# Weights of each dense phase of a hybrid decoder trunk land in up to 16 places, and PE waits for them piece by piece in a first tile written apart

## The chip, the cores and the metric

The kernel runs on one core of one Trainium2 chip. The metric is the device time of one execution in microseconds; before the change the median of three runs is 3684.71 us (3683.56 to 3687.84).

## What is computed

One inference step of a two-layer decoder trunk, for a prompt of 2048 rows and a sample group of 8x8 rows with the same weights, all in float32. With D = 1024, cut to what matters:

```python
for i in range(2):
    u = rms_norm(h, norm_w[i])
    if i == 0:
        z = u @ w_in_even            # 1024 x 4616: q, k, v, forget, rq, rk, rv, gate
        m = even_out(fox_attention(z), retention(z), gate) @ w_out_even
    else:
        xb, g = split(u @ w_in_odd)  # 1024 x 2048
        m = (rg_lru(conv(xb)) * silu(g)) @ w_out_odd
    h = h + m
    e = rms_norm(p[i] @ ple_proj[i], ple_norm_w[i])
    h = h + sigmoid(h @ ple_gate_w[i]) * e
y = rms_norm(h, final_norm_w)
```

The outputs are y, the new keys, values and forget values, and the new retention, recurrent and convolution states.

## The kernel before, in words

The trunk runs phase after phase, with a barrier of all engines between two: the input projection in two halves (`in_proj`, tiles named `in`), sample retention, attention, retention, the tail of layer 0 (`tail`), the recurrent layer (`lru`), and the tail of layer 1. The order within a phase is the order in which each engine's code is written; there is no scheduler. SP issues nearly all transfers, from one queue.

Rows are worked through in T = 17 tiles of 128 (16 of the prompt, one of the sample). `each_tile` (L101) runs a step for each: a hardware loop over pairs of tiles, then the last three (in the second half seven) written out. `lru` is written out whole, in groups of 512 rows, the sample's 64 rows first.

Every float32 product is made of three: the operands are cut into a high and a low part, and `split3` (L125 to L127) adds high by high, high by low and low by high. The weights are cut on the chip by `SplitWeights` (L130). A piece is 128 rows by 512 columns, 256 KB. SP loads piece n into place n modulo the number of places, and first waits until the piece that was there has been cut (L149); ACT writes the high part (`make_high`, L154), DVE the low part (`make_low`, L159) and counts `low`, on which PE waits. In `in_proj` there are four column groups of eight pieces, so 32, and eight places; in the tail of layer 0 the projection and output weights are held from earlier and the 16 gate pieces use four places lent by `u_hi` and `u_lo`; in the tail of layer 1 there are 4 + 16 + 16 pieces and six places; in `lru` 16 pieces and eight places at the start (later ones come during the run).

In tile 0 of `in_proj` PE takes the groups in turn and for each waits for all eight of its pieces. In the first half, x must first be normalised (`norm`, by ACT and DVE), turned (`turn`, L692, by PE through `ps_t`) and cut; tile t+1 is normalised by ACT and DVE at the head of step t, and turned by PE between groups 1 and 2. Group 2 there also holds the eight forget columns, which ACT and DVE cut last of all (`wf_split`). The first matmul group of a tile needs the bank that the evacuation of the tile before has emptied: in the second half DVE's rotary (L642 to L647) empties group 0's. There POOL multiplies the last gate by `gn`, and side work on forget values (`GatesAside`) has constants of its own.

In the tails DVE adds the output product to h (`add_out`, L2421) after it has cut the first eight gate pieces, and PE turns the sum (L2515). In `lru` ACT works out a softplus of lambda (L2787 to L2791), which needs the constants, before it cuts weights; then it copies the sample's rows (`keep_rows`, L2798), PE turns them, and `keep` (L2805) takes up the first channel block.

## Time and profile before

| | |
|---|---|
| median of the timed runs | 3684.71 us (3683.56 to 3687.84) |
| the profiled execution | 3673.12 us |
| its span, first to last instruction | 3671.4 us |
| PE busy | 3268.0 us (89%), 22374 matmuls |
| DVE, ACT, POOL busy | 1719.6, 1281.3, 294.9 us |
| HBM traffic | 172 GB/s over the span |
| mean granted PE clock | 0.943 |

The profile is of one execution; its span leaves out 1.7 us around the first and the last instruction. PE is the matmul engine, PEld its weight loads, DVE, ACT and POOL the elementwise engines, SPq the queue from which SP issues transfers. PEclk is the clock that was granted to PE as a share of full speed. A window's busy time is what an engine worked in that stretch; where a row ends in brackets, they hold the engine's idle time before it and what ended it.

### The profile page before, as it was taken

Reading aid. Unit: us, or ns where it says so; the run is one execution under the profiler, and the core shown is the slowest. Engines: PE = TensorE matmul, PEld = TensorE weight load, DVE = VectorE, ACT = ScalarE, POOL = GpSimd, SP = SyncE. Lnnn points to the kernel's source line nnn. Section 1 sums busy time; section 2 is a strip of 40 time slices with the busy share of each in tenths; the row PEclk is TensorE's granted clock in tenths of the full one; section 3 lists DMA queues with packets and bytes.
Section 4 is the critical chain, followed back from the end, with each engine's and each line's share of the span. In section 5 each row is a group of like instructions: output and inputs, shape, how many; then the busy total and the mean of one; then the engine's idle time right before and its main releaser. Section 6 shows DMA issues by size and latency. Waiting matters only on the chain. (4 is left out here: it accounts for less than half of the span.)

```text
span 3671.4 us, 63114 instructions
## 1 busy us (share of the span) xinstructions
PE 3268.0 (89%) x22374; PEld 2483.7 (68%) x22374; DVE 1719.6 (47%) x2974; ACT 1281.3 (35%) x2326; POOL 294.9 (8%) x306
## 2 busy tenths in 40 slices
PE   6999789996699999999996859999869999499998
PEld 5888678884465565556554747888757677378887
DVE  3222231142776677667652753333346676433333
ACT  3111121120134334334333533333356666533232
POOL 0000000011211111111100530000000000000000
PEclk9999899996699999999998979999989999699999
DMA  5444652344688898789866863333244433332221
GB/s 146 139 139 139 192 138 93 108 140 123 221 289 287 271 316 282 266 285 320 282 216 205 292 240 120 113 121 123 98 170 138 129 132 106 120 116 89 80 89 59
DMA packets 381250, 636.26 MB, mean 173 GB/s; under 512 B 138697, under 2 KB 201201, under 8 KB 364594
## 3 DMA queue, kind: packets, MB, share of 16 engines
q1 hardware_dynamic: 361730, 496.54, 41.0%
q0 software_dynamic: 19264, 136.46, 10.6%
q8 instruction: 143, 2.34, 0.3%
q14 instruction: 113, 0.93, 0.1%
HBM read 488.74 MB, written 144.13 MB: 172 GB/s over the span
## 5 line engine op out<-in xcount | busy, mean ns | idle before, releaser
L125 PE MATMUL in_ps_z<-in_w_hi,in_u_hi 128*128 128x512 f32 x952 | 374.9, 394 | 43.3 <-DVE in_w_lo L159 43.3
L126 PE MATMUL in_ps_z<-in_w_lo,in_u_hi 128*128 128x512 f32 x952 | 373.4, 392 | 0.0
L127 PE MATMUL in_ps_z<-in_w_hi,in_u_lo 128*128 128x512 f32 x952 | 373.2, 392 | 0.0
L1521 DVE STREAM_TRANSPOSE att_samp_kt<-att_samp_k_ring 128x1024 f32<-128x1024 f32 x256 | 306.9, 1225 | 24.5 <-DMA att_samp_k_ring<-cache_k,att_samp_rows_now 12.3
L1676 PE MATMUL att_fox_ps_o<-att_fox_prob,att_fox_v_one 128*65 128x512 f32 (+3 forms) x640 | 290.3, 537 | 10.1 <-ACT att_fox_prob L1377 9.8
L1377 ACT ACTIVATE att_fox_prob<-att_fox_ps_k 128x512 f32<-128x512 f32 (+1 forms) x320 | 167.4, 531 | 243.0 <-DVE att_fox_ps_k L1489 156.5
L125 PEld LDWEIGHTS in_ps_z<-in_w_hi,in_u_hi 128*128 128x128 f32 x952 | 180.6, 190 | 82.3 <-issue 28.7
L125 PE MATMUL tail_ps_g<-tail_wg_hi,tail_h_hi 128*128 128x512 f32 x544 | 216.5, 398 | 13.9 <-DVE tail_p_lo L2405 9.8
L1470 DVE TENSOR_REDUCE att_fox_part_max<-att_fox_ps_n 128x1 f32<-128x512 f32 (+2 forms) x320 | 193.4, 604 | 72.1 <-PE att_fox_ps_n L1643 63.0
L127 PE MATMUL tail_ps_g<-tail_wg_hi,tail_h_lo 128*128 128x512 f32 x544 | 212.9, 391 | 0.0
L126 PE MATMUL tail_ps_g<-tail_wg_lo,tail_h_hi 128*128 128x512 f32 x544 | 212.9, 391 | 0.0
L127 PEld LDWEIGHTS in_ps_z<-in_w_hi,in_u_lo 128*128 128x128 f32 x952 | 180.6, 190 | 38.0
L126 PEld LDWEIGHTS in_ps_z<-in_w_lo,in_u_hi 128*128 128x128 f32 x952 | 180.7, 190 | 36.9
L1302 POOL DMA_INDIRECT att_samp_k_ring<-cache_k,att_samp_rows_now x128 | 121.0, 946 | 750.6 <-DVE att_samp_kt L1521 683.7
L2433 DVE SCALAR_TENSOR_TENSOR tail_e<-tail_ps_g,tail_e 128x512 f32<-128x512 f32 x68 | 47.0, 692 | 278.7 <-ACT tail_ps_g L2366 278.7
L1660 PE MATMUL att_fox_ps_k<-att_fox_q_a,att_fox_k_a 128*128 128x512 f32 (+1 forms) x320 | 167.6, 524 | 9.4 <-issue 7.1
L1733 PEld LDWEIGHTS att_samp_ps_v<-att_samp_v_ring,att_samp_prob_t 128*16 128x16 f32 x4096 | 102.7, 98 | 74.2 <-issue 65.0
L1707 PE MATMUL att_samp_ps_s<-att_samp_kt,att_samp_q_blocks 128*32 128x128 f32 x4096 | 149.2, 290 | 0.0
L1707 PEld LDWEIGHTS att_samp_ps_s<-att_samp_kt,att_samp_q_blocks 128*32 128x32 f32 x4096 | 111.5, 115 | 50.9 <-issue 48.7
L1733 PE MATMUL att_samp_ps_v<-att_samp_v_ring,att_samp_prob_t 128*16 128x128 f32 x4096 | 140.8, 279 | 4.0 <-DMA att_samp_v_ring<-cache_v 4.0
L1642 PE MATMUL att_fox_ps_n<-att_fox_k_a,att_fox_q_a 128*128 128x512 f32 (+2 forms) x320 | 127.0, 397 | 19.3 <-DVE att_fox_part_max L1470 16.0
L125 PEld LDWEIGHTS tail_ps_g<-tail_wg_hi,tail_h_hi 128*128 128x128 f32 x544 | 102.7, 189 | 48.1 <-DVE tail_h_lo L2426 21.3
(385 smaller groups left out, 6835.9 us busy)
## 6 DMA issues: line engine op xcount, KB each, us to landing
att_samp_v_ring<-cache_v SPq DMA_DIRECT2D x512, 256.0 KB
tail_a_hi<-a_hi SPq DMA_DIRECT2D x34, 512.0 KB, 5.9
tail_a_lo<-a_lo SPq DMA_DIRECT2D x34, 512.0 KB, 6.2
in_w_stage<-w_in_even SPq DMA_DIRECT2D x64, 256.0 KB, 6.7
lru_u_hi<-u_hi SPq DMA_DIRECT2D x8, 2048.0 KB, 8.0
lru_u_lo<-u_lo SPq DMA_DIRECT2D x8, 2048.0 KB, 13.0
in_x<-x SPq DMA_DIRECT2D x17, 512.0 KB, 3.5
u_hi<-in_u_hi SPq DMA_DIRECT2D x17, 512.0 KB, 3.8
```

Of the source, the lines that this page charges most:

```text
L125: pe.matmul(out, act_hi, w_hi, start=start, stop=False)
L126: pe.matmul(out, act_hi, w_lo, start=False, stop=False)
L127: return pe.matmul(out, act_lo, w_hi, start=False, stop=stop)
L1302: pool.indirect_dma_start(k_ring[:, n % KR, :], None, io["cache_k"], bass.IndirectOffsetOnAxis(ap=rows_now[:, par, n:n + 1], axis=0)).then ...
L1377: act.activation(prob[:, s % 4, r:G], ps_k[:, s % 2, r:G], ACT.Exp).then_inc(exped.sem, 1)
L1470: dve.tensor_reduce(part_max[:, g, b % B4, c:c + 1], ps_n[:, 0:w], AX.X, ALU.max).then_inc(maxed.sem, 1)
L1521: ins = dve.transpose(kt[:, n % 2, :, :].rearrange("p c (s i) -> p s c i", s=SLOTS)[:, p * two:(p + 1) * two], k_ring[:, n % KR, p * two * ...
L1642: pe.matmul(ps_n[:, 0:w], q_a[:, par, q], k_a[:, par, k], start=True, stop=False)
L1660: pe.matmul(ps_k[:, s % 2, r:G], k_a[:, par, k], q_a[:, par, q], start=True, stop=False)
L1676: pe.matmul(ps_o[0:HD + 1, r:G], v[:, par, kt, :], prob[:, s % 4, r:G], start=kt == 0, stop=kt == B4 * (g + 1) - 1).then_inc(weighed.sem, 1)
L1707: last = pe.matmul(ps_s[h * QUAD:(h + 1) * QUAD, at:at + PAGE], q_blk[:, bpar, block, :], kt[:, y, block, :], start=False, stop=y == 1 and ...
L1733: last = pe.matmul(acc[a * QUAD:a * QUAD + 2 * NS, :], prob_t[:, c % 2, at:at + 2 * NS], v_ring[:, y, p, a * P:(a + 1) * P], start=c == 0 ...
```

## The change

It does the following, in the five dense phases:

- `in_proj`: the weights get 16 places instead of 8. In the first half 12 are their own and four are the buffer `z`, in the second eight are their own and eight are `z`, `gate_half` and `gate_tanh`. ACT and DVE wait for all pieces (`all_made`) before they write these buffers.
- SP issues tile 0's rows ahead of the constants, tile 1's rows after the first eight pieces, and gn and the side work's constants last. b_forget gets its own semaphore.
- Tile 1's norm is done by ACT and DVE after the first 16 pieces.
- PE waits for each piece by itself in tile 0, and no more in later tiles. For that, PE's tiles 0 and 1 are written apart, ahead of the loop (`apart=1`); in the first half ACT's and DVE's too.
- `tail`: identity and p first, with the identity on its own semaphore; the two norm weights after tile 0's rows; in layer 0 six places for the gate weights instead of four; PE's waits per piece, and tiles 0 and 1 apart.
- `lru`: 16 places, eight of them working buffers; rows first, then all 16 pieces, then the constants; the weights are cut ahead of the softplus; the later pieces count on semaphores of their own.

The core of the diff:

```diff
@@ each_tile
-def each_tile(eng, step, tiles=T, unroll=2, peel=3):
+def each_tile(eng, step, tiles=T, unroll=2, peel=3, apart=0):
-    with eng.Fori(0, pairs) as i:
+    for t in range(2 * apart):
+        step(t, t // 2, t % 2)
+    with eng.Fori(apart, pairs) as i:
@@ SplitWeights
+    def all_made(self, eng):
+        eng.wait_ge(self.low, len(self.pieces))
@@ in_proj
-        weights = SplitWeights(ph, pieces, 8)
+        idle = [z[:, g, :] for g in range(GN)] + ([] if first else [b[:, g, :] for b in (half_z, tanh_z) for g in range(2)])
+        weights = SplitWeights(ph, pieces, 12 if first else 8, idle)
@@ in_proj, sync
-            if first:
-                sp.dma_start(ident[:, :], io["identity"]).then_inc(consts_in, 16)
-                sp.dma_start(nw[:, :], io["norm_w"][0:1, :].broadcast_to([P, D])).then_inc(consts_in, 16)
-                sp.dma_start(bf[:, :], io["b_forget"][0:1, :].broadcast_to([P, H])).then_inc(consts_in, 16)
-            else:
-                sp.dma_start(gn[:, :], io["ret_gn_w"][0:1, :].broadcast_to([P, W])).then_inc(consts_in, 16)
...
             fetch(0, 0)
+            if first:
+                sp.dma_start(nw[:, :], io["norm_w"][0:1, :].broadcast_to([P, D])).then_inc(consts_in, 16)
+                sp.dma_start(ident[:, :], io["identity"]).then_inc(consts_in, 16)
             weights.load(sp, 0, KC)
+            fetch(1, 1)
+            weights.load(sp, KC, 2 * KC)
+            if first:
+                sp.dma_start(bf[:, :], io["b_forget"][0:1, :].broadcast_to([P, H])).then_inc(bf_in, 16)
+                sp.dma_start(wf_st[:, :, :], w_in[:, :, 3 * W:3 * W + H]).then_inc(wf_in, 16)
+            weights.load(sp, 2 * KC, GN * KC)
             if not first:
+                sp.dma_start(gn[:, :], io["ret_gn_w"][0:1, :].broadcast_to([P, W])).then_inc(consts_in, 16)
                 side.load(sp)
-            fetch(1, 1)
-            if first:
-                sp.dma_start(wf_st[:, :, :], w_in[:, :, 3 * W:3 * W + H]).then_inc(wf_in, 16)
-            weights.load(sp, KC, GN * KC)
@@ in_proj, scalar
-            weights.make_high(act, 0, GN * KC)
+            weights.make_high(act, 0, 2 * KC)
+            if first:
+                norm(1, 0, 1)
+            weights.make_high(act, 2 * KC, GN * KC)
             if first:
                 split_forget_act(act)
-            each_tile(act, step, peel=PEEL)
+            weights.all_made(act)
+            each_tile(act, step, peel=PEEL, apart=int(first))
@@ in_proj, vector
-            weights.make_low(dve, 0, GN * KC)
+            weights.make_low(dve, 0, 2 * KC)
+            if first:
+                norm(1, 0, 1)
+            weights.make_low(dve, 2 * KC, GN * KC)
             if first:
                 split_forget_dve(dve)
-            each_tile(dve, step, peel=PEEL)
+                dve.wait_ge(bf_in, 16)
+            weights.all_made(dve)
+            each_tile(dve, step, peel=PEEL, apart=int(first))
@@ in_proj, tensor
+            def piece_made(t, g, k):
+                if isinstance(t, int) and t == 0:
+                    pe.wait_ge(weights.low, g * KC + k + 1)
             def group(t, par, g):
-                pe.wait_ge(weights.low, (g + 1) * KC)
...
                     for k in range(KC):
+                        piece_made(t, g, k)
-            each_tile(pe, step, peel=PEEL)
+            each_tile(pe, step, peel=PEEL, apart=1)
@@ tail
-            gate_weights = SplitWeights(ph, more, 0, us)
+            gate_weights = SplitWeights(ph, more, 2, us)
...
-            for dst, src in [(ident[:, :], io["identity"]), (nw_e[:, :], io["ple_norm_w"][layer:layer + 1, :].broadcast_to([P, D])),
-                             (nw_u[:, :], next_w.broadcast_to([P, D]))]:
-                sp.dma_start(dst, src).then_inc(consts_in, 16)
...
             fetch_p(0, 0)
+            sp.dma_start(ident[:, :], io["identity"]).then_inc(ident_in, 16)
             fetch_p(1, 1)
             if not kept:
                 weights.load(sp, 0, PROJ)
             fetch(0, 0)
+            fetch_norms()
@@ tail, vector
-            dve.wait_ge(consts_in, 48)
...
+            dve.wait_ge(consts_in, 32)
             norm_e(0, 0, 0)
@@ tail, tensor
-            pe.wait_ge(consts_in, 48)
+            pe.wait_ge(ident_in, 16)
-                    if not kept:
-                        pe.wait_ge(weights.low, PROJ + (g + 1) * KC)
                     for k in range(KC):
+                        if not kept and isinstance(t, int) and t == 0:
+                            pe.wait_ge(weights.low, PROJ + g * KC + k + 1)
...
-            each_tile(pe, step)
+            each_tile(pe, step, apart=1)
@@ lru
-        weights = SplitWeights(ph, pieces, 8)
+        weights = SplitWeights(ph, pieces, LB, [b[:, 0:G] for b in (tr, ti, tg, th, sq, q, root, bx)])
...
-            sp.dma_start(chan[:, :, 0:8], io["channel"]).then_inc(consts_in, 16)
-            for n, name in enumerate(["gate_r_w", "gate_i_w"]):
-                sp.dma_start(gates[:, n], io[name][0:BH].rearrange("b d e -> d b e")).then_inc(consts_in, 16)
-            sp.dma_start(ident[:, :], io["identity"]).then_inc(consts_in, 16)
-            sp.dma_start(past_x[:, :, :, :], io["past_x"]).then_inc(consts_in, 16)
-            sp.dma_start(past_h[:, :, :], io["past_h"]).then_inc(consts_in, 16)
...
-            weights.load(sp, 0, 4)
             fetch(0, 0)
-            weights.load(sp, 4, 2 * KC)
+            weights.load(sp, 0, 2 * KC)
+            sp.dma_start(ident[:, :], io["identity"]).then_inc(consts_in, 16)
+            sp.dma_start(chan[:, :, 0:8], io["channel"]).then_inc(consts_in, 16)
+            sp.dma_start(past_x[:, :, :, :], io["past_x"]).then_inc(consts_in, 16)
+            sp.dma_start(past_h[:, :, :], io["past_h"]).then_inc(consts_in, 16)
+            for n, name in enumerate(["gate_r_w", "gate_i_w"]):
+                sp.dma_start(gates[:, n], io[name][0:BH].rearrange("b d e -> d b e")).then_inc(consts_in, 16)
             fetch(1, 1)
@@ lru, scalar
+            weights.make_high(act, 0, 2 * KC)
             act.wait_ge(consts_in, 96)
...
-            weights.make_high(act, 0, 2 * KC)
+            keep_rows(0)
             act.wait_ge(ready, 2)
-            keep_rows(0)
+            weights.all_made(act)
             keep(0, 0, 0, 0)
@@ lru, vector
+            weights.make_low(dve, 0, 2 * KC)
             dve.wait_ge(consts_in, 96)
...
-            weights.make_low(dve, 0, 2 * KC)
@@ lru, tensor
-                    pe.wait_ge(weights.low, (n + 1) * KC if t == 0 else 4 * KC)
+                    if t:
+                        pe.wait_ge(weights.low, 4 * KC)
                     for k in range(KC):
+                        if t == 0:
+                            pe.wait_ge(weights.low, n * KC + k + 1)
```

Three places in the order of the instructions. SP, start of the first half of the input projection, before (`in_w_stage` is the places of their own, `in_x` and `in_cos_sin` a tile's rows, `in_wf_stage` the forget columns):

```order
L494 DMA in_ident<-identity 128x128
L495 DMA in_norm_w<-norm_w 128x1024
L496 DMA in_b_forget<-b_forget 128x8
L503 DMA in_x<-x 128x1024
L507 DMA in_cos_sin<-cos_sin 128x64
L149 DMA in_w_stage<-w_in_even 128x512 x8
L503 DMA in_x<-x 128x1024
L507 DMA in_cos_sin<-cos_sin 128x64
L515 DMA in_wf_stage<-w_in_even 128x8x8
L149 DMA in_w_stage<-w_in_even 128x512 [waits in0_w_low_made] x24
```

and now:

```order
L508 DMA in_cos_sin<-cos_sin 128x64
L512 DMA in_norm_w<-norm_w 128x1024
L513 DMA in_ident<-identity 128x128
L151 DMA in_w_stage<-w_in_even 128x512 x8
L504 DMA in_x<-x 128x1024
L508 DMA in_cos_sin<-cos_sin 128x64
L151 DMA in_w_stage<-w_in_even 128x512 x4
L151 DMA in_z<-w_in_even 128x512 x4
L518 DMA in_b_forget<-b_forget 128x8
L519 DMA in_wf_stage<-w_in_even 128x8x8
L151 DMA in_w_stage<-w_in_even 128x512 [waits in0_w_low_made] x12
L151 DMA in_z<-w_in_even 128x512 [waits in0_w_low_made] x4
```

Tile 0's x (L504) stands ahead of these; sixteen pieces are issued before the first that waits, where there were eight. ACT in the same place, from the cut of tile 0's u on, before:

```order
L572 CAST in_u_hi<-in_ps_t 128x1024
L154 CAST in_w_hi<-in_w_stage 128x512 x16
L154 CAST in_wv_hi<-in_w_stage 128x512 x8
L154 CAST in_w_hi<-in_w_stage 128x512 x8
L550 CAST in_wv_hi<-in_wf_stage 128x8x8
```

and now:

```order
L579 CAST in_u_hi<-in_ps_t 128x1024
L159 CAST in_w_hi<-in_w_stage 128x512 x12
L159 CAST in_w_hi<-in_z 128x512 x4
L570 ACTIVATE in_ps_t,in_stat<-in_x 128x1024
L572 ACTIVATE in_stat<-in_stat 128x1
L159 CAST in_wv_hi<-in_w_stage 128x512 x8
L159 CAST in_w_hi<-in_w_stage 128x512 x4
L159 CAST in_w_hi<-in_z 128x512 x4
L557 CAST in_wv_hi<-in_wf_stage 128x8x8
```

The two instructions of tile 1's norm (L570, L572) now stand after the sixteenth piece; before, they came in the loop behind the forget columns. ACT at the start of the recurrent layer, before:

```order
L2787 ACTIVATE lru_soft<-lru_channel 128x8
L2789 ACT_TABLE_LOAD
L2789 ACTIVATE lru_soft<-lru_soft 128x8
L2791 ACT_TABLE_LOAD
L2791 ACTIVATE lru_soft<-lru_soft 128x8
L154 CAST lru_w_hi<-lru_w_stage 128x512 x16
L2798 COPY lru_new_rows<-lru_ps_x 64x512
L2798 COPY lru_new_rows<-lru_ps_g 64x512
L2805 COPY lru_xb<-lru_ps_x 128x8x8
```

and now, from the last three pieces on:

```order
L159 CAST lru_w_hi<-lru_minus_one_less 128x512
L159 CAST lru_w_hi<-lru_root 128x512
L159 CAST lru_w_hi<-lru_gated_x 128x512
L2817 ACTIVATE lru_soft<-lru_channel 128x8
L2819 ACT_TABLE_LOAD
L2819 ACTIVATE lru_soft<-lru_soft 128x8
L2821 ACT_TABLE_LOAD
L2821 ACTIVATE lru_soft<-lru_soft 128x8
L2828 COPY lru_new_rows<-lru_ps_x 64x512
L2828 COPY lru_new_rows<-lru_ps_g 64x512
L2835 COPY lru_xb<-lru_ps_x 128x8x8
```

The casts of the sixteen pieces now come ahead of the softplus, and the row copies behind it.

## Rows read from the trace of the kernel before

**Rows 1.** Part 1 of the page: busy us (share of the span), instructions.
```profile
PE 3268.0 (89%) x22374; PEld 2483.7 (68%) x22374; DVE 1719.6 (47%) x2974; ACT 1281.3 (35%) x2326; POOL 294.9 (8%) x306
```

**Rows 2.** Windows, first half's start: stretch, length, PE, PEld, DVE, ACT, POOL, PEclk, DMA, GB/s.
```profile
7.00:15.00 8.00, 1.94 (x8) 1.57 (x8) 1.60 (x3) 2.66 (x5) 0.00 (x0) 1.00 1.00 363
15.00:19.00 4.00, 0.00 (x0) 0.00 (x0) 2.98 (x5) 4.00 (x7) 0.00 (x0) 1.00 0.11 24
19.00:31.00 12.00, 8.54 (x24) 6.48 (x24) 7.22 (x12) 5.11 (x10) 0.00 (x0) 1.00 0.97 172
31.00:37.00 6.00, 3.75 (x16) 3.11 (x17) 5.03 (x8) 4.96 (x9) 0.00 (x0) 1.00 1.05 390
37.00:47.00 10.00, 1.98 (x9) 1.31 (x7) 5.86 (x9) 5.19 (x9) 0.00 (x0) 0.75 1.01 186
```

**Rows 3.** Timelines of DVE and PE there: start us, us, operation [idle before <-releaser].
```profile
48.27 0.69 DVE L159 TENSOR_TENSOR in_w_lo<-in_w_stage,in_w_hi 128x512 fp32r<-128x512 f32 x1 [0.44 <-ACT in_w_hi L154]
...
51.64 1.97 PE L692 MATMUL in_ps_t<-in_ident,in_xn 128*128 128x128 f32 x8 [12.65 <-DVE in_xn L624]
...
54.05 0.42 PE L125 MATMUL in_ps_z<-in_wv_hi,in_u_hi 128*128 128x260 f32 x1
54.27 0.42 PE L126 MATMUL in_ps_z<-in_wv_lo,in_u_hi 128*128 128x260 f32 x1
...
57.53 0.28 PE L127 MATMUL in_ps_f<-in_wv_hi,in_u_lo 128*128 128x260 f32 x1
57.65 0.28 PE L125 MATMUL in_ps_f<-in_wv_hi,in_u_hi 128*128 128x260 f32 x1
```

**Rows 4.** Windows, start of the projection's second half, columns as in rows 2.
```profile
439.00:442.00 3.00, 0.00 (x0) 0.00 (x0) 0.00 (x0) 0.00 (x0) 0.00 (x0) 0.50 0.93 156
442.00:447.00 5.00, 0.00 (x0) 0.00 (x0) 0.00 (x0) 0.52 (x1) 0.00 (x0) 0.50 1.04 389
...
457.00:468.00 11.00, 4.14 (x15) 3.01 (x14) 4.16 (x6) 3.71 (x6) 0.00 (x0) 0.81 1.02 163
468.00:474.00 6.00, 3.30 (x8) 2.63 (x9) 4.58 (x7) 4.79 (x8) 0.00 (x0) 0.50 1.05 381
474.00:486.00 12.00, 10.07 (x42) 7.93 (x40) 6.88 (x11) 5.75 (x10) 0.00 (x0) 0.94 0.97 171
```

**Rows 5.** Timelines of SP, PE and DVE there.
```profile
452.44 25.76 SPq L149 DMA_DIRECT2D in_w_stage<-w_in_even  x24
...
487.53 0.50 PE L125 MATMUL in_ps_z<-in_w_hi,in_u_hi 128*128 128x512 f32 x1 [3.46 <-DVE in_w_lo L159]
...
489.15 0.42 DVE L647 TENSOR_TENSOR in_z<-in_prod_cos,in_prod_sin 128x256 f32<-128x256 f32 x1
```

**Rows 6.** Timelines of PE and DVE, start of layer 0's tail; DMA issues (median to landing).
```profile
2210.22 0.49 PE L125 MATMUL tail_ps_g<-tail_wg_hi,tail_h_hi 128*128 128x512 f32 x1 [2.57 <-DVE tail_wg_lo L159]
...
2190.88 1.34 DVE L159 TENSOR_TENSOR tail_wg_lo<-tail_u_hi,tail_wg_hi 128x512 fp32r<-128x512 f32 x2 [0.58 <-ACT tail_wg_hi L154]
...
2197.26 1.33 DVE L159 TENSOR_TENSOR tail_wg_lo<-tail_u_lo,tail_wg_hi 128x512 fp32r<-128x512 f32 x2 [0.90 <-ACT tail_wg_hi L154]
...
tail_u_hi<-ple_gate_w SPq DMA_DIRECT2D x8, 256.0 KB, 3.2
```

**Rows 7.** Windows and timelines of ACT at the start of the recurrent layer.
```profile
2709.00:2722.00 13.00, 13.00 (x56) 10.74 (x56) 3.95 (x22) 5.84 (x13) 0.00 (x0) 0.92 0.94 345
...
2671.07 0.22 ACT L2787 ACTIVATE lru_soft<-lru_channel 128x8 f32<-128x8 f32 x1 [11.80 <-DMA lru_past_h<-past_h]
...
2674.24 1.64 ACT L154 CAST lru_w_hi<-lru_w_stage 128x512 fp32r<-128x512 f32 x3
...
2697.11 0.21 ACT L2805 COPY lru_xb<-lru_ps_x 128x64 f32<-128x64 f32 x1
```

**Rows 8.** Timeline of PE at the start of layer 1's tail.
```profile
3224.87 1.97 PE L2515 MATMUL tail_ps_t<-tail_ident,tail_h 128*128 128x128 f32 x8 [5.76 <-DVE tail_h L2421]
```

**Rows 9.** Part 3 of the page: DMA queue, kind: packets, MB, share of 16 engines.
```profile
q8 instruction: 143, 2.34, 0.3%
```

More of the change, by code:

```diff
@@ L575, in step @@
                 if first and not static(t + 1, LAST):
-                    norm(t + 1, i + par, 1 - par)
+                    if not (isinstance(t, int) and t == 0):
+                        norm(t + 1, i + par, 1 - par)
                     cut(t + 1, i + par, 1 - par)
@@ L650, in step @@
                 if first and not static(t + 1, LAST):
-                    norm(t + 1, i + par, 1 - par)
+                    if not (isinstance(t, int) and t == 0):
+                        norm(t + 1, i + par, 1 - par)
                     cut(t + 1, i + par, 1 - par)
@@ L2290, in _, with fetch_norms @@
             next_w = io["norm_w"][1:2, :] if first else io["final_norm_w"]
-            for dst, src in [(ident[:, :], io["identity"]), (nw_e[:, :], io["ple_norm_w"][layer:layer + 1, :].broadcast_to([P, D])),
-                             (nw_u[:, :], next_w.broadcast_to([P, D]))]:
-                sp.dma_start(dst, src).then_inc(consts_in, 16)
+            def fetch_norms():
+                for dst, src in [(nw_e[:, :], io["ple_norm_w"][layer:layer + 1, :]), (nw_u[:, :], next_w)]:
+                    sp.dma_start(dst, src.broadcast_to([P, D])).then_inc(consts_in, 16)
             def fetch_p(t, par):
@@ L2526, in gate @@
                             pe.wait_ge(*h1_low.at(t, k // 4))
+                        if isinstance(t, int) and t == 0:
+                            pe.wait_ge(gate_weights.low, OUT + g * KC + k + 1 - gate_base)
                         last = split3(pe, ps_g[:, g, :], t_hi[:, k * P:(k + 1) * P], t_lo[:, k * P:(k + 1) * P], half(wg_hi[:, k, :], g),
@@ L2614, in lru @@
         y = ph.sb("y", [P, G])
+        weights = SplitWeights(ph, pieces, LB, [b[:, 0:G] for b in (tr, ti, tg, th, sq, q, root, bx)])
+        later_in = [ph.sem(f"w_later_in{x}") for x in range(LB)]
         y_hi = ph.sb("y_hi", [P, 2, G], F32R)
```

26 lines of the change are left out of this document (15 added, 11 removed).

## The prediction

> **What bounds the kernel now.** I read the busy shares first. [rows 1] PE computes in 89% of the span, and nothing the diff touches changes how many matmuls there are or how long one takes. What can move is PE's idle time, and the edits sit at the starts of five phases, between barriers, so I went to the windows, engine timelines and waits of those starts and worked out each phase's saving by itself; a barrier keeps them apart, so they add.
>
> First half of the input projection: the DMA engines are full from 7 to 15 us, then nearly empty for 4 us (24 GB/s), because eight places hold eight pieces and SP may not issue the ninth until DVE has cut the first [rows 2]. DVE cuts the last piece at 48.27, only then come tile 1's norm and its turn (51.64), and PE starts group 2 right behind it, at 53.26, two matmuls before the 54.05 of [rows 3]. One more thing in [rows 2] shapes everything: with the engines equally full (share 0.97 to 1.05) pieces 8 to 15 and 24 to 31 arrive at 172 to 186 GB/s, pieces 16 to 23 at 390. The second half shows the same pattern: 163, 381, 171 [rows 4]. It is not the number of places: there pieces 8 to 15 could all be issued at once from 452.44 (DVE had cut the first eight by then) and still ran at 163. So a piece of an odd column group costs about 1.45 us, one of an even group 0.67, and more places do not shorten that.
>
> **The change, part by part.**
>
> *Input projection, first half.* The bytes ahead of piece 8 stay the same (x, norm weights, identity, eight pieces, second x); with 16 places piece 8 follows at once. The empty stretch goes: 19 minus 15 is 4 us, less 0.3 for the small b_forget and forget columns that now stand among the pieces, 3.7. All later pieces are paced by their transfer, so the last cut moves from 48.96 (48.27+0.69) to 45.3. Second, tile 1's norm and turn now happen after piece 15: before, PE waited for them from the cut of the forget columns, done 0.1 to 0.2 us after the last piece's, to 53.26: 4.2 us [rows 3]. Group 2 still waits for `wf_split`, which ACT and DVE reach only after all 32 pieces, so the waits per piece give nothing to groups 2 and 3, and finishing groups 0 and 1 sooner only lengthens PE's idle time before them. Its price: PE was already 1.6 us into its warm-up when group 2 began (turn from 51.64); now group 2 begins cold. A 260-column matmul follows the last after 0.22 us at the 1.2 GHz level (54.05, 54.27) and after 0.12 at 2.4 GHz (57.53, 57.65) [rows 3], so 1.6 us of it costs 0.8. Sum 3.7+4.2-0.8 = **7.1 us** (bounds 5 and 10: no warm-up help at all and a slower restart of the queue; or x, now first, bringing everything 3 us forward).
>
> *Input projection, second half.* Bytes ahead of piece 8 fall: before, gn 0.26, u 1.08, eight pieces 2.10, the side work's constants 0.85 and second u 1.08 MB, 5.4 MB, ending at 457 [rows 4]; after, 4.26 MB, at the 389 GB/s of 442 to 447 from 439.2 on, ends at 450.1. That is 6.9 us, and the rest of the stream is paced by transfer. gn and constants go behind the pieces; POOL needs gn only for the store of group 3, and fetch(2), queued behind it on SP, is wanted only by tile 2, a tile's 96 matmuls of 0.23 us or 22 us later. Then PE: group 3 now runs piece by piece. Before, it started at 487.53 and tile 1 followed 5.6 us later. After, PE is done about 1 us after the last cut, but tile 1's group 0 waits for the bank that DVE's rotary empties, 2.1 us after the last cut (to 489.57) [rows 5]. So 5.6-2.2 = 3.4 us. I take off 1.0 for a colder start of tile 1: in the first half PE worked from 51.64 on, was still at the slow pace at 54.27 and at the quick one at 57.53 [rows 3]; half of the time between is lost, 1.3 to 2.9, say 2, and I give it one chance in two. 6.9+3.4-1.0 = **9.3 us** (6 to 13).
>
> *Tail of layer 0.* Identity and p come ahead of 1 MB of norm weights, so PE starts some 4 us sooner; but that is not the limit. The turn of h1 waits for add_out on DVE, which stands behind the cut of the eighth gate piece, done at 2198.6 (2197.26+1.33), and with four places the fifth to eighth came late [rows 6]. With six, two more come without a gap, and the last two are issued at the first two cuts (2191.5 and 2192.2, from 2190.88 on) and land 3.2 us later by the median of such issues: 2195.4, cast 0.6, cut 0.7, 2196.7, so 1.9 us. The 2.57 us that PE waited for the second half of the gate weights [rows 6] goes too: six pieces lie ready behind the turn. Against it: PE, done with out_proj 4 us sooner, idles some 3.6 us before the turn. In its 12.65 us of idle time before 51.64 [rows 3] the clock fell to the 1.2 GHz level: the mean 0.75 of 37 to 47 [rows 2] puts that near 42, after 3 us. I charge 0.7. **3.8 us** (1.5 to 6).
>
> *Recurrent layer.* Before: consts, four pieces, u, then pieces at eight places, and the first keep at 2697.11, right behind the copy of g's rows [rows 7]. After: 1.05 MB of u and 4.2 MB of pieces run without a gap, at the 389 GB/s of [rows 4] from 2667.2 (1.6 us after the first issue) to 2680.7; the last is cut near 2682.3. PE follows per piece, done by 2683. Now the consts are late: 0.7 MB in short rows, landing about 2684. ACT then needs 3.2 us for the three small activations with two table loads (2671.07 to the first cast at 2674.24), and 1.1 for both row copies: first keep at 2688.6. **8.5 us** (5 to 10). What was hidden beside the loads, the softplus chain, is now in the open; without that it would be 12.
>
> *Tail of layer 1.* Places stay six and bytes ahead of w_out stay 3.8 MB. PE's early start ends in the same wait: DVE cuts the eighth gate piece, then add_out (5.76 us of waiting for PE), then the turn at 3224.87 [rows 8]. **0** (-2 to 3).
>
> Straight-line tiles 0 and 1 lengthen PE's code by a seventh (5895 rows to 6771), but add no instruction that runs. I price them at 0: all of the recurrent layer is straight-line already, and from 2709 to 2722 PE is busy in 13.00 of 13.00 us with the DMA engines at 0.94 [rows 7]. Waits of ACT and DVE on all pieces are met when they are reached; the lent buffers are first written after them.
>
> Sum: 7.1+9.3+3.8+8.5 = 28.7 us. The profiled execution took 3673.1 us and would take 3644.4; the median of the three timed runs is 3684.7, 11.6 above it, so I forecast **3656.0**.
>
> **A rule against the change.** Fed per piece, PE gets 3 matmuls (0.69 us at full pace) every 1.45 us. Before, between whole groups, it idled 12.65 us and the clock fell to half anyway [rows 2, 3]. The Trainium skill (TensorE: Matmul & The Clock Gate, HAM oscillation) describes a kernel whose every K tile started at half clock because each waited for its transfer, and advises running all K tiles before waiting again. By that rule the first tiles stay at 1.2 GHz; rival B is what it would do here, worked out from rows. No row yet shows PE fed at this pace.
>
> **Rivals.**
> A. More places raise the transfer rate, and 172 GB/s was a matter of waiting. For: the empty stretches vanish exactly there. Against: the full share, and the back-to-back issue at 452.44. Then DVE paces at 0.69 per piece. In the first half it starts near 15.5 (x, now first, brings it 1.7 us forward) and loses 3 to tile 1's norm: last cut 15.5+32x0.69+3 = 40.6. In the second the first piece lands near 444.3 (446.48, ACT's 0.52 us in the stretch to 447 [rows 4], less 2.2 for gn and the slow 439 to 442): 444.3+0.7+22 = 467. Gain (48.96-40.6)+4.2-0.8, (487.5-467)+3.4, 3.8 and 8.5, about 48: 3637. Beside it: the Trainium skill (HBM Reference, Specifications and Access) gives a core streaming alone about 425 GB/s, which the even groups approach and the odd ones do not. Chance 0.08.
> B. PE at half clock through each first tile. A matmul of 512 columns then takes 0.22x512/260 = 0.43 [rows 3], a piece 1.28: hidden at 1.45, not at 0.67. Second half: group 2 loses 3.6, tile 1 starts cold, 1 more; recurrent layer: 16x1.28 = 20.5 from the first cut near 2672, 4.5 lost; tail 0: turn and half the gate, 2.5. Gain 28.7-11.6 = 17: 3668. Chance 0.09.
> C. Slower. PE's code comes by DMA: 143 packets, 2.34 MB on queue 8 [rows 9], 16 KB each. If a block queues behind all places, it waits 16x1.45 = 23 us; once in each of three starts, 70-29 = 41 slower: 3726. It decides from a stall of 10 us per start. Against it [rows 7], as above. Chance 0.04.
> D. The gains are swallowed by a later wait, for instance the second and third tiles' inputs. Against: each such fetch hangs on tile 0's own results, so it moves with it. 3685. Chance 0.05.
>
> **How the numbers follow.** The forecast has 0.74. Its bounds taken together (the deviations are independent) give a gain of 20 to 39; B widens it to 17, part of A to 42: 3643 to 3669. About 0.2%, 7.4 us, is what a measurement of this kernel tells from nothing: faster by more 0.74+0.08+0.09 = 0.91, within 0.05, slower 0.04.
>
> **What would show it.** Right: no stretch under 100 GB/s between 7 us and the last piece; group 2 of the first half starting near 45.5; tile 1 of the second half about 9 us sooner; the stall before the second gate half in tail 0 gone; the first keep of the recurrent layer waiting on the consts and not on PE; tail 1 unchanged at its turn. Wrong: rates of the odd groups near 390 (A); the granted clock 0.5 through tile 0 and 1 (B); idle time of PE in tile 1 put down to issue (C).

## The result, and the profile after

The changed kernel takes 3655.9 us, the median of six runs (3652.7 to 3669.8), against 3684.5 before (3680.4 to 3687.8): a ratio of 0.9927, 95% interval 0.9912 to 0.9943, or 21 to 32 us. The forecast was 3656.0. The busy shares of the page, to be held against [rows 1] and [rows 9]:

```profile
PE 3279.9 (90%) x22374; PEld 2490.2 (68%) x22374; DVE 1719.5 (47%) x2974; ACT 1281.2 (35%) x2326; POOL 295.4 (8%) x306
...
q8 instruction: 153, 2.51, 0.3%
```

PE's count is the same. It is busy 12 us longer, which tells nothing yet: a second profile of the kernel before had 3285.4 us, 17 more than the first.

The total is the weakest evidence here. The profiled execution of the changed kernel spans 3654.6 us, 16.8 less than that of before, where the medians differ by 28.7. So I read each phase by itself, from SP's first issue in it to the first issue of the next. In the changed kernel these are:

```profile
429.84 0.34 SPq L506 DMA_DIRECT2D in_u_hi<-u_hi  x1
...
831.87 0.56 SPq L808 DMA_DIRECT2D prep_natural<-rq  x1
...
2161.74 0.35 SPq L2321 DMA_DIRECT2D tail_p<-p  x1
...
2652.71 0.34 SPq L2748 DMA_DIRECT2D lru_u_hi<-u_hi  x1
...
3166.63 0.34 SPq L2321 DMA_DIRECT2D tail_p<-p  x1
```

The table has the lengths in us. "Mean" is over all profiles whose code was the same in that phase: two of before, four to six with the changed kernel's code. The column of gains is the difference of the two means.

| phase | before, first profile | after, first profile | mean before | mean after | gain | forecast |
|---|---|---|---|---|---|---|
| input projection, first half | 438.1 | 429.8 | 438.1 | 430.0 | 8.1 | 7.1 |
| second half | 411.9 | 402.0 | 413.1 | 402.6 | 10.5 | 9.3 |
| sample retention to retention | 1324.3 | 1329.9 | | | | |
| tail of layer 0 | 491.2 | 491.0 | 491.7 | 489.5 | 2.1 | 3.8 |
| recurrent layer | 518.5 | 513.9 | 520.5 | 514.9 | 5.6 | 8.5 |
| tail of layer 1 | 487.3 | 488.0 | 488.3 | 488.9 | -0.6 | 0 |

The five gains add to 25.7, inside the interval of the timed runs. The stretch in the middle has the same instructions in all kernels and took between 1322 and 1340 us in the thirteen profiles. That is the noise of this kernel. It is 5.6 us of the 11.9 by which the two single profiles (16.8) fall short of the medians (28.7); most of the rest is that the first profile of before was also quick in its dense phases.

**First half.** Windows of the changed kernel, for [rows 2], columns as there:

```profile
11.00:15.00 4.00, 0.95 (x6) 0.58 (x4) 2.06 (x3) 3.10 (x6) 0.00 (x0) 1.00 1.01 330
15.00:19.00 4.00, 4.00 (x10) 3.13 (x11) 4.00 (x8) 2.69 (x5) 0.00 (x0) 1.00 1.04 182
19.00:23.00 4.00, 4.00 (x16) 3.17 (x15) 1.97 (x3) 1.38 (x3) 0.00 (x0) 1.00 1.04 151
...
27.00:31.00 4.00, 2.69 (x9) 1.45 (x9) 2.98 (x6) 3.34 (x7) 0.00 (x0) 1.00 1.06 364
...
35.00:39.00 4.00, 0.00 (x0) 0.00 (x0) 3.39 (x6) 2.07 (x4) 0.00 (x0) 0.50 0.99 175
```

The empty stretch is gone, and the pattern of slow (151 to 182 GB/s) and quick (364) column groups is as it was. Timelines of DVE and PE there, for [rows 3]:

```profile
42.78 1.36 DVE L164 TENSOR_TENSOR in_w_lo<-in_z,in_w_hi 128x512 fp32r<-128x512 f32 x2
44.06 0.22 DVE L561 TENSOR_TENSOR in_wv_lo<-in_wf_stage,in_wv_hi 128x64 fp32r<-128x64 f32 x1
...
31.73 1.10 PE L710 MATMUL in_ps_t<-in_ident,in_xn 128*128 128x128 f32 x8 [1.31 <-DVE in_xn L636]
44.38 0.56 PE L127 MATMUL in_ps_z<-in_wv_hi,in_u_hi 128*128 128x260 f32 x1 [11.55 <-issue]
```

The last piece is cut at 44.14 (42.78+1.36), 4.8 us sooner than before; group 2 follows the cut of the forget columns at once. PE idled 11.55 us ahead of it; the trace puts that down to "issue", but the cut that ends just before shows the wait.

**Second half.** Windows and PE's timeline, for [rows 4, 5]:

```profile
445.00:450.00 5.00, 2.56 (x11) 1.52 (x10) 1.90 (x3) 1.24 (x2) 0.00 (x0) 1.00 1.02 185
450.00:455.00 5.00, 3.87 (x9) 2.24 (x9) 2.08 (x3) 2.19 (x4) 0.00 (x0) 0.58 1.01 238
455.00:461.00 6.00, 5.97 (x21) 4.85 (x22) 5.67 (x9) 5.51 (x10) 0.00 (x0) 0.78 1.05 391
461.00:466.00 5.00, 4.89 (x22) 3.70 (x21) 3.15 (x5) 2.23 (x4) 0.00 (x0) 1.00 0.98 190
...
470.18 0.50 PE L127 MATMUL in_ps_z<-in_w_hi,in_u_hi 128*128 128x512 f32 x1 [0.37 <-DVE in_w_lo L164]
474.79 0.47 PE L127 MATMUL in_ps_z<-in_w_hi,in_u_hi 128*128 128x512 f32 x1 [1.55 <-DVE in_z L659]
```

Group 3 follows its pieces, and tile 1 begins when the rotary has emptied its bank (L659), as forecast: 44.95 us after the phase's start, where it was 55.

**Tail of layer 0.** PE's timeline and the windows around it, for [rows 6]; ahead of them the turn in the kernel before:

```profile
2199.84 1.10 PE L2515 MATMUL tail_ps_t<-tail_ident,tail_h 128*128 128x128 f32 x8 [1.75 <-DVE tail_h L2421]
```

```profile
2187.01 1.97 PE L2542 MATMUL tail_ps_t<-tail_ident,tail_h 128*128 128x128 f32 x8 [4.67 <-DVE tail_h L2447]
2189.72 0.77 PE L127 MATMUL tail_ps_g<-tail_wg_hi,tail_h_hi 128*128 128x512 f32 x1 [0.75 <-DVE tail_h_lo L2452]
...
2185.74:2189.74 4.00, 1.98 (x9) 1.61 (x9) 2.02 (x5) 1.31 (x3) 0.00 (x0) 0.50 0.61 210
2189.74:2193.74 4.00, 4.00 (x10) 3.17 (x11) 4.00 (x7) 2.97 (x6) 0.00 (x0) 0.50 0.37 127
2193.74:2197.74 4.00, 4.00 (x16) 3.25 (x15) 1.53 (x3) 2.52 (x3) 0.00 (x0) 0.84 0.12 37
```

The stall of 2.57 us between the gate's halves is gone, and yet the phase gained 0.2 in this profile. PE idled 4.67 us ahead of the turn, where it was 1.75; the clock stands at 0.50 through the turn, which took 1.97 us (1.10 before), and through most of the gate's first half.

**Recurrent layer.** ACT's timeline, for [rows 7]:

```profile
2660.85 5.37 ACT L159 CAST lru_w_hi<-lru_w_stage 128x512 fp32r<-128x512 f32 x8 [14.43 <-DMA lru_w_stage<-w_in_odd]
...
2673.73 0.22 ACT L2817 ACTIVATE lru_soft<-lru_channel 128x8 f32<-128x8 f32 x1 [2.02 <-DMA lru_gate_w<-gate_i_w]
...
2677.97 0.21 ACT L2835 COPY lru_xb<-lru_ps_x 128x64 f32<-128x64 f32 x1
```

The first keep hangs on the constants and the chain behind them, as forecast. It comes 25.3 us after the phase's start; before it was 31.5.

**Tail of layer 1**, PE's timeline, for [rows 8]: still the wait for `add_out`, now with 10.31 us of idle time ahead of it.

```profile
3209.13 1.97 PE L2542 MATMUL tail_ps_t<-tail_ident,tail_h 128*128 128x128 f32 x8 [10.31 <-DVE tail_h L2447]
```

### The profile page after: what moved, and what is told of

Same layout as the page of the kernel before. It is cut to its first block and busy times, and to the rows that moved or that the text cites. A ratio compares the mean times of both kernels' runs of the same rounds, so it can differ in the third digit from the quotient of the medians.

```text
span 3654.6 us, 62896 instructions
## 1 busy us (share of the span) xinstructions
PE 3279.9 (90%) x22374; PEld 2490.2 (68%) x22374; DVE 1719.5 (47%) x2974; ACT 1281.2 (35%) x2326; POOL 295.4 (8%) x306
## 5 line engine op out<-in xcount | busy, mean ns | idle before, releaser
L127 PE MATMUL in_ps_z<-in_w_hi,in_u_hi 128*128 128x512 f32 x952 | 376.3, 395 | 25.7 <-DVE in_w_lo L164 24.0
L1665 PE MATMUL att_fox_ps_n<-att_fox_k_a,att_fox_q_a 128*128 128x512 f32 (+2 forms) x320 | 127.8, 399 | 18.6 <-DVE att_fox_part_max L1493 15.1
```

Source lines behind the costliest of these rows:

```text
L127: pe.matmul(out, act_hi, w_hi, start=start, stop=False)
L1665: pe.matmul(ps_n[:, 0:w], q_a[:, par, q], k_a[:, par, k], start=True, stop=False)
```

## The experiments

All but two start from the changed kernel. Since barriers part the phases, one kernel can hold edits in several. "First output" of a tail is SP's first issue of a result of tile 0, counted from the phase's start: 44.4 and 45.3 in the two profiles of before for layer 0, 44.4 and 42.9 in the two of the changed kernel.

### The kernel before, once more

> The kernel before once more, for a second profile. The profiled execution of before was 11 us under its median. If that was a quick passage of the attention phase (in the trace of before the stretch from the start of sample retention to the start of layer 0's tail took 1324.3 us, in the changed kernel 1329.9 with the same instructions), this profile shows the five dense phases within 1 us each of the first (438.1 for the first half of the projection, 411.9 for the second, 491.2 for layer 0's tail, 518.5 for the recurrent layer, 487.3 for layer 1's tail) and the stretch between anywhere from 1320 to 1340. If instead the dense phases themselves vary by several us, the savings read phase by phase are not to be trusted.

Measured: 3687.4 us, in one run. Phases 438.1, 414.2, 492.1, 522.5, 489.4, the middle 1329.4. The first half is the same to 0.1, but the other dense phases are 0.9 to 3.9 us longer, so the 1 us that I expected was too narrow: of the 14.3 us between the two profiles 9.2 lie in the dense phases and 5.1 in the middle. A single profile shows a gain of 5 us in a phase, not one of 2; for smaller ones I use marks close to the edit, and means.

### Places as before

```diff
-        weights = SplitWeights(ph, pieces, 12 if first else 8, idle)
+        weights = SplitWeights(ph, pieces, 8)
...
-            gate_weights = SplitWeights(ph, more, 2, us)
+            gate_weights = SplitWeights(ph, more, 0, us)
...
-        weights = SplitWeights(ph, pieces, LB, [b[:, 0:G] for b in (tr, ti, tg, th, sq, q, root, bx)])
+        weights = SplitWeights(ph, pieces, LB)
```

> The changed kernel with the numbers of places of before (8, 8, 4, 8). Theory: places matter only where they close an empty stretch. First half of the projection: the ninth piece waits for the first cut, the stretch comes back, +3.7 to 4.8. Second half: the second tile's rows cover the wait, 0 to +1. Layer 0's tail: the gate pieces come in at the rate of the transfer, with six places as with four, 0. Recurrent layer: the constants now queue on SP behind pieces that wait for cuts, so the first keep comes 2 to 4 later. Sum +6 to +10, about 3664. Rival: places raise the rate at which pieces arrive; then the second half loses 5 or more as well and the sum is over 14.

Measured: 3662.1 us (ratio to the kernel before 0.9929, 0.9907 to 0.9952). First half 435.4, so +5.4 to the mean; second half 404.1, +1.5; layer 0's tail 490.2, +0.7; recurrent layer 515.6, its first keep at 26.2, which is the mean of six profiles with sixteen places (26.1). Windows and PE of the first half:

```profile
11.00:15.00 4.00, 0.95 (x4) 0.58 (x4) 2.29 (x3) 3.33 (x6) 0.00 (x0) 1.00 0.70 243
15.00:19.00 4.00, 4.00 (x10) 3.12 (x10) 3.75 (x7) 1.84 (x4) 0.00 (x0) 1.00 0.76 132
...
49.51 0.56 PE L127 MATMUL in_ps_z<-in_wv_hi,in_u_hi 128*128 128x260 f32 x1 [14.28 <-issue]
```

The DMA share falls to 0.70 and group 2 starts 5.1 us later. So the places are worth 5 us in the first half and little elsewhere. In the recurrent layer I had the mechanism wrong: SP did issue the constants 4 us later, but they landed at 22.0 us, where sixteen places gave 20.8 to 22.5, since the bytes ahead of them are the same and the stream had no gap to close.

### Whole groups

```diff
-                    pe.wait_ge(weights.low, g * KC + k + 1)
+                    pe.wait_ge(weights.low, (g + 1) * KC)
```

and likewise in both tails and the recurrent layer.

> The changed kernel with PE waiting for all eight pieces of a group, as before, all else kept. Theory: nothing in the first half (group 2 waits for the forget columns anyway), +3 in the second half (group 3 starts at the last cut, 5.2 of matmuls, of which the rotary's 2.2 were waited for anyway), 0 in layer 0's tail, +0.5 to 1 in the recurrent layer, 0 to +1 in layer 1's tail. Sum +4 (3 to 5). Rival: the waits per piece are what saves in every phase; then the first half loses 3 or more too and the sum is over 8. A second rival: PE fed per piece stays cool and whole groups are quicker; then the second half gains.

Measured: 3659.7 us (0.9923, 0.9906 to 0.9941). First half 429.5, no change; second half 404.2, +1.6; layer 0's tail 489.7, no change; recurrent layer's first keep at 28.3, +2.2; layer 1's tail 488.2. The first rival falls with the first half. The waits per piece are worth some 4 us, in these two phases alone. Both sizes were missed: +3 was expected in the second half, where tile 1 began 47.24 us after the phase's start instead of 44.9 to 46.5, and 0.5 to 1 in the recurrent layer. In the recurrent layer PE now began only with the eighth piece, after 20.76 us of idle time, at half clock, and ACT waited for it:

```profile
2677.57 0.58 ACT L2828 COPY lru_new_rows<-lru_ps_g 64x512 f32<-64x512 f32 x1 [3.28 <-PE lru_ps_g L129]
```

### Norms back

```diff
             weights.make_high(act, 0, 2 * KC)
-            if first:
-                norm(1, 0, 1)
             weights.make_high(act, 2 * KC, GN * KC)
...
+            fetch_norms()
             fetch_p(0, 0)
             sp.dma_start(ident[:, :], io["identity"]).then_inc(ident_in, 16)
...
             fetch(0, 0)
-            fetch_norms()
```

The first edit also in DVE, with the norm again in the loop's first step; the second in both tails.

> The changed kernel with tile 1's norm back in the loop (first half of the projection) and the two norm weights again ahead of identity and p (both tails). Theory for the first: group 2 starts 4.1 later (the 4.2 of the prediction), phase +4. Theory for layer 0's tail, where the change gained 0.3 instead of 3.8: PE's work on the output projection was moved early by 4 us while the turn of h1 stayed where it was, so PE idled 4.67 us ahead of it instead of 1.75, its clock fell, and the turn took 1.97 instead of 1.10 us and the gate's first half 8 instead of 6. With the norm weights ahead again PE stays at full clock: phase 2 to 3.5 us shorter. Rival: the missing 3.5 us lie in the gate pieces' arrival, and the order of the norm weights does nothing (within 0.7). Layer 1's tail: within 1.

Measured: 3657.0 us (0.9916, 0.9898 to 0.9935). The first half takes 434.0, +4.0: the norm's term of the sum, 4.2, is confirmed. Layer 0's tail takes 487.4, 2.1 less than the mean, and its first output comes at 40.8. PE and its windows there (the phase begins at 2160.62):

```profile
2185.20 1.09 PE L2534 MATMUL tail_ps_t<-tail_ident,tail_h 128*128 128x128 f32 x8 [0.78 <-DVE tail_h L2439]
2187.46 0.47 PE L127 MATMUL tail_ps_g<-tail_wg_hi,tail_h_hi 128*128 128x512 f32 x1 [1.17 <-DVE tail_h_lo L2444]
...
2180.62:2184.62 4.00, 3.79 (x17) 2.81 (x15) 2.15 (x4) 1.13 (x2) 0.00 (x0) 1.00 0.94 309
2184.62:2188.62 4.00, 2.26 (x13) 1.87 (x14) 2.63 (x5) 2.73 (x6) 0.00 (x0) 1.00 0.24 81
2188.62:2192.62 4.00, 4.00 (x20) 3.29 (x19) 3.48 (x6) 2.48 (x5) 0.00 (x0) 1.00 0.53 164
```

PE starts 4 us later, and the phase is shorter. The idle time ahead of the turn is 0.78 us, the clock stays at 1.00, the turn takes 1.09, and the gate's matmuls run at full pace. A phase that is 2 us shorter in one profile would not be enough, but the mark is: from the turn to the first output it took 16.2 us here, and 18.1 to 19.1 in the seven profiles with identity and p first and tile 1's rows in their old place. In all seven the clock fell to 0.50, for some 7 us in six and 10 in the first, behind waits of 3.1 to 5.9 us ahead of the turn. In one of them the turn itself was still quick, and the gate's matmuls were not (0.63 us each):

```profile
2183.34 1.09 PE L2542 MATMUL tail_ps_t<-tail_ident,tail_h 128*128 128x128 f32 x8 [4.16 <-DVE tail_h L2447]
```

So in layer 0's tail bringing identity and p forward moved PE's work away from the wait that it could not pass, and cooled it.

### Forget columns early

```diff
             if first:
                 norm(1, 0, 1)
+                split_forget_act(act)
             weights.make_high(act, 2 * KC, GN * KC)
-            if first:
-                split_forget_act(act)
```

and the same in DVE.

> The changed kernel with the forget columns cut right after tile 1's norm, behind sixteen pieces instead of behind all 32, in the first half of the projection. In the changed kernel PE stood idle 11.55 us ahead of group 2, waiting for them, with the last piece cut at 44.13. Theory: group 2 now runs beside the cutting and group 3 piece by piece, done 1 us behind the last cut; tile 1 starts when its rows are cut, near 46.6 instead of 57.2: phase 10 us shorter (8.5 to 11). Rival: PE, fed a piece every 1.45 us, is at half clock when tile 1 begins and the gain is 1.5 to 3 less. A second rival: the forget columns themselves land late, group 2 still waits, gain under 3.

Measured: 3647.3 us (0.9897, 0.9878 to 0.9917). The first half takes 419.1 us, 10.9 less. PE's timeline:

```profile
31.43 1.10 PE L709 MATMUL in_ps_t<-in_ident,in_xn 128*128 128x128 f32 x8 [1.29 <-DVE in_xn L635]
...
46.40 0.50 PE L127 MATMUL in_ps_z<-in_w_hi,in_u_hi 128*128 128x512 f32 x1 [1.07 <-DVE in_u_lo L641]
```

Groups 2 and 3 run beside the cutting and tile 1 begins at 46.40, at full clock. The rivals fall.

### Channel table first

```diff
+            sp.dma_start(chan[:, :, 0:8], io["channel"]).then_inc(chan_in, 16)
             fetch(0, 0)
             weights.load(sp, 0, 2 * KC)
             sp.dma_start(ident[:, :], io["identity"]).then_inc(consts_in, 16)
-            sp.dma_start(chan[:, :, 0:8], io["channel"]).then_inc(consts_in, 16)
```

ACT and DVE wait for `chan_in` alone and work out the softplus ahead of their cuts.

> The changed kernel with the recurrent layer's channel table issued first, on a semaphore of its own, and the softplus worked out ahead of the cuts, while the weights are on their way. In the changed kernel the constants landed 21.0 us after the phase's start and the chain of three activations and two table loads stood in the open behind them; PE was done with both groups of rows at 22.6. Theory: the first keep (25.3 us after the phase's start in the profile of the change, 26.8 in a later profile of the same code) comes 2 us sooner. Rival: the other constants or PE's own work are the limit and it moves by less than 0.7.

Measured: 3650.7 us (0.9922, 0.9905 to 0.9938). The phase begins at 2645.27, so the first keep is at 23.1, 3.0 sooner than the mean of 26.1. ACT and PE:

```profile
2648.24 0.21 ACT L2817 ACTIVATE lru_soft<-lru_channel 128x8 f32<-128x8 f32 x1 [9.26 <-DMA lru_channel<-channel]
...
2668.32 0.22 ACT L2836 COPY lru_xb<-lru_ps_x 128x64 f32<-128x64 f32 x1 [0.47 <-PE lru_ps_x L3020]
...
2667.88 0.27 PE L3020 MATMUL lru_ps_x<-lru_ident,lru_new_rows 64*128 64x64 f32 x1 [0.64 <-DMA lru_gate_w<-gate_i_w]
```

The softplus is hidden again. What is late next shows too: the last of the constants, the gate weights, landed 22.6 us after the phase's start, and PE waited 0.64 us for them.

### Tile 1's rows later

```diff
-            fetch(1, 1)
-            gate_weights.load(sp, OUT - gate_base, GATE - gate_base)
+            gate_weights.load(sp, OUT - gate_base, OUT + KC - gate_base)
+            fetch(1, 1)
+            gate_weights.load(sp, OUT + KC - gate_base, GATE - gate_base)
```

> The changed kernel with the rows of tile 1 (1.5 MB) issued behind the first eight gate pieces instead of ahead of them, in both tails. Theory: the turn of h1 hangs on the cut of the eighth gate piece, so 1.5 MB less ahead of it, near 390 GB/s, brings it some 3.5 to 4 us forward; in layer 0's tail PE then idles 1 us instead of 4.7 ahead of the turn and keeps its clock. First tile's output asked for 4 to 6 us sooner in layer 0's tail (44.4 in the profile of the change), 3 to 5 sooner in layer 1's (65.1). Rival: tile 1's rows are then late for the output product behind the first gate, and it all comes back there, within 1.

Measured: 3649.8 us (0.9906, 0.9889 to 0.9924). Layer 0's tail takes 484.9, 4.7 less, its first output at 38.3; layer 1's 485.1, 3.8 less, first output at 62.3 instead of 65 to 67. PE in layer 0's tail, which begins at 2164.21:

```profile
2186.35 1.10 PE L2543 MATMUL tail_ps_t<-tail_ident,tail_h 128*128 128x128 f32 x8 [1.57 <-DVE tail_h L2448]
```

The turn comes 22.1 us after the start instead of 24 to 25 and at full clock. The rows of tile 1 were not late.

### Columns exchanged

```diff
-        pieces = [(io["w_in_even"][0, k * P:(k + 1) * P, starts[g]:starts[g] + G], *weight(g, k)) ...]
+        pieces = [(io["w_in_even"][0, k * P:(k + 1) * P, starts[g ^ 1]:starts[g ^ 1] + G], *weight(g, k)) ...]
```

> The changed kernel with the weights of groups 0 and 1, and of 2 and 3, exchanged in both halves of the projection: each group reads the columns of its neighbour, so q, k, v and so on come out in each other's place. It asks what makes every second group arrive at 163 to 186 GB/s. If it is the columns (where a row's 2 KB lie in memory), the first and the third group are now the slow ones, and the first and third stretches of the windows show it. If it is the place in the stream (how much is in flight, the slots used), the second and fourth are slow as before. The times of the phases hardly move in either case, save that a slow first group delays PE's first tile.

Measured: 3654.6 us, in one run, every phase within its spread; its outputs stand in each other's place, as intended. Windows of the first half:

```profile
11.00:15.00 4.00, 1.16 (x6) 0.75 (x4) 1.76 (x3) 2.81 (x5) 0.00 (x0) 1.00 1.04 165
...
19.00:23.00 4.00, 4.00 (x16) 3.22 (x16) 2.05 (x4) 2.47 (x4) 0.00 (x0) 1.00 1.06 400
...
27.00:31.00 4.00, 2.86 (x16) 1.99 (x14) 3.34 (x7) 2.33 (x6) 0.00 (x0) 1.00 1.03 159
...
35.00:39.00 4.00, 0.00 (x0) 0.00 (x0) 2.79 (x5) 2.81 (x6) 0.00 (x0) 0.50 1.02 376
```

The slow stretches are now the first and the third, the quick ones the second and the fourth, and in the second half of the projection it is the same. So it is the columns, and not the place in the stream.

### The loop's first tiles apart, alone

```diff
-    with eng.Fori(0, pairs) as i:
+    for t in range(2 * apart):
+        step(t, t // 2, t % 2)
+    with eng.Fori(apart, pairs) as i:
```

on the kernel before, with `apart` as in the change.

> The kernel before with nothing changed but that PE's first two tiles (in the first half of the projection ACT's and DVE's too) are written out ahead of the loop. The prediction prices the longer code at nothing: every phase within 1 us of the two profiles of the kernel before, the recurrent layer and attention within their own spread of 4 and 6. Rival C of the prediction: code blocks queue behind weights, 10 us or more in each of the three starts.

Measured: 3687.2 us in one run. Phases 437.8, 414.3, 494.6, 522.4, 487.7, against 438.1, 414.2, 492.1, 522.5, 489.4 of the kernel before's second profile. Nothing of the size of rival C. Layer 0's tail is 2.5 longer: PE waited 2.65 us between the gate's halves there, as before (2.57 and 2.50), but came out of it with its first matmul at 0.79 us instead of 0.49, so at half clock. That is outside the 1 us that was expected, and one profile doesn't tell whether the written-out code has a part in it; the prediction's price of nothing is shown for the projection and stays open here.

### All three edits together, and the changed kernel again

> The changed kernel with the three edits that helped, together: forget columns cut after sixteen pieces, channel table and softplus first in the recurrent layer, tile 1's rows behind the first eight gate pieces in both tails. Measured apart, by their phases' marks: 10.8, 3, 4 and 3.5 us. If phases add, some 21 us under the changed kernel, a ratio to the kernel before of 0.987 where the changed kernel's is 0.992 to 0.993. Rival: gains of neighbouring phases overlap or the attention phase takes some back; under 15 us.

> The changed kernel, unchanged, on the same chip as the runs beside it, so that the combined version stands against it directly: ratio 0.991 to 0.994 to the kernel before. Its profile gives the phases' marks once more: first half 429 to 431, first keep 25 to 27 us after its phase's start, layer 0's tail with its turn of h1 at half clock (about 2 us).

Measured on one chip, against 3682.4 us for the kernel before: the changed kernel 3656.9 (0.9930, 0.9916 to 0.9943), the three edits together 3633.4 (0.9869, 0.9854 to 0.9885). So they take another 23.5 us off. Phases 421.8, 401.8, 484.9, 511.7, 485.1: 8.2, 4.6, 3.2 and 3.8 less than the changed kernel's means in the four that were edited, some 20 together. The first half gave 8.2 and not 10.9. The row of PE at the start of tile 1, and the window after it:

```profile
47.54 0.76 PE L127 MATMUL in_ps_z<-in_w_hi,in_u_hi 128*128 128x512 f32 x1 [1.43 <-DVE in_u_lo L641]
...
46.00:51.00 5.00, 3.57 (x9) 2.78 (x9) 3.91 (x8) 1.12 (x3) 0.00 (x0) 0.66 0.01 3
```

With the same code as in the run above (46.40, clock 1.00), PE waited twice (0.99 us at 45.14, 1.43 here) and the clock went down. Which side it falls to differs between the two profiles, and what decides it is not shown.

## Why the prediction was right

*The total.* 3656.0 was forecast and 3655.9 measured, which is closer than the terms deserve, and luck: they were 1.0, 1.2, -1.7, -2.9 and -0.6 off, cancel only in part, and leave the phases 3.0 us short of the 28.7 that the medians give. The range of 3643 to 3669 is the honest measure. One step of its working doesn't come out: the terms' own bounds, taken as independent (the root of the sum of squares), give a gain of 23 to 35, not 20 to 39; the range rests on B and A.

*First half, 7.1, measured 8.1.* Both terms hold. The empty stretch was put at 3.7; the last cut came 4.8 sooner, and taking the places away cost 5.1 at group 2. The norm and turn of tile 1 were put at 4.2, and taking them back cost 4.0. The cold start was charged 0.8: group 2 began 8.9 us sooner (44.38 instead of 53.26) and the phase is 8.1 to 8.3 shorter, so 0.6 to 0.8 went that way. That the waits per piece give nothing here holds too (429.5 with whole groups).

*Second half, 9.3, measured 10.5.* The bytes ahead of piece 8 were to bring the last cut forward by 6.9; it went from 49.4 to 42.3 us after the phase's start, 7.1. Group 3 by piece and the bank: forecast tile 1 2.1 us behind the last cut, measured 2.65 (472.14 to 474.79). The 1.0 for a cold tile 1 was not needed: the clock was 1.00 from 461 on.

*Tail of layer 0, 3.8, measured 2.1.* The step that failed is the clock, charged at 0.7. Without it the working gives 1.9+2.6 = 4.5, and with PE kept busy up to the turn the phase was 4.3 shorter than before. With the change as it is it was 2.1 shorter: the clock costs 2.1 (489.5 less 487.4), three times the charge. I had charged the idle time for the turn and the start of the gate; the windows show half clock for some 7 us in six profiles and 10 in the first.

*Recurrent layer, 8.5, measured 5.6.* The chain was right, a size off. (Its own sum, 2684+3.2+1.1, is 2688.3 and not 2688.6.) The constants were to land 18.4 us after the phase's start (2684); ACT, which waits for them, began the softplus at 20.8 to 22.5 in eight profiles, and from there to the first keep it took the 4.3 that were forecast, except with whole groups. With them 2.4 to 4.1 us later, the first keep came at 25.3 to 26.8 instead of 23.0. The term that was mis-sized is the stream: the estimate put 5.25 MB at 389 GB/s from 1.6 us after the start on, and the first six us moved only 199 to 238 GB/s:

```profile
2652.70:2655.70 3.00, 0.00 (x0) 0.00 (x0) 0.10 (x2) 0.00 (x0) 0.00 (x0) 0.50 0.67 238
2655.70:2658.70 3.00, 0.00 (x0) 0.00 (x0) 0.00 (x0) 0.00 (x0) 0.00 (x0) 0.50 0.75 199
2658.70:2661.70 3.00, 0.00 (x0) 0.00 (x0) 0.20 (x1) 0.78 (x2) 0.00 (x0) 0.50 0.97 332
...
2667.70:2670.70 3.00, 3.00 (x14) 1.75 (x13) 3.00 (x5) 2.77 (x5) 0.00 (x0) 1.00 1.15 299
2670.70:2673.70 3.00, 3.00 (x14) 1.75 (x13) 1.69 (x3) 0.89 (x2) 0.00 (x0) 1.00 0.88 231
```

Added up from these windows (399 and 390 GB/s in the two left out), 5.25 MB had moved some 16.9 us after the start, where the estimate had 15.1, and the constants came 4.1 us behind that instead of 3.3. Why the start is slow is not shown.

*Tail of layer 1, 0, measured -0.6*, within its spread. PE's early start ends in the same wait.

*Rivals.* A, that more places raise the rate, is out: 151 to 190 GB/s in the slow groups with sixteen places. B, half clock through the first tiles, is out for most of it: at 15 to 27 us PE was fed a slow group piece by piece and the clock stood at 1.00. In the second half it fell to half for some 7 us (0.58 in 450 to 455, 0.78 in 455 to 461) behind a wait of 2.39 us, in the slow group and on into the quick one; the slow group behind that gave the time back, since PE was waiting for a piece again at 470.18. The rule of the Trainium skill (TensorE: Matmul & The Clock Gate, HAM oscillation), that K tiles which each wait for a transfer start cold, holds here for a few pieces and not for all. What cost time was another wait, PE's 4.67 us for DVE's sum in layer 0's tail. C is out: the code grew by 10 packets on queue 8, and written out alone it cost nothing in the projection. D is out by the first and second tiles' marks, which kept their lead to the phases' ends in the projection. In the recurrent layer the first keep came 6.3 us sooner in the first profile and the phase ended 4.6 sooner, but by the means it is 5.4 and 5.6: nothing was lost.

## What to carry to other kernels

Bring forward only what the next unavoidable wait depends on. Work that is moved early and then waits at the same place gains nothing, and can lose, since PE can go to half clock while it waits (here behind waits of 3.1 us and more): layer 0's tail was 2 us shorter with PE starting 4 us later. More landing places pay where the transfers stand idle for want of one (5 us in one phase of the five here) and nowhere else; and once a stream is continuous, what counts is the order of the bytes and which small thing (forget columns, a channel table) stands behind all of it.
